# Two-layer hybrid decoder: retention products from rounded parts, and a reordered first feed-forward chunk

## The reference, cut to what matters

```
for i in range(2):
    x += mixer_i(rms_norm(x))                  # i = 0: retention, i = 1: attention
    x += relu(rms_norm(x) @ W_up)**2 @ W_down  # 1024 -> 4096 -> 1024

# retention, for each of 4 heads (q, k: 256 features, v: 512), in chunks of C = 128 tokens
scores = einsum('bnihd,bnjhd->bnhij', qc, kc) * dmat      # within a chunk
intra  = einsum('bnhij,bnjhe->bnihe', scores, vc)         # scores times v
def step(S, xs):
    cross = einsum('bihd,bhde->bihe', qi * q_dec, S)      # q times the state
    S = S * c_dec + einsum('bjhd,bjhe->bhde', ki * k_dec, vi)   # k times v
o = intra + cross;  o = o * rsqrt(mean(o*o) + eps);  o = o * silu(g);  return o @ w_out, S
```

## Time and profile before

| What | Value |
|---|---|
| Median of 3 executions | 2858.24 us |
| The profiled execution | 2859.83 us |
| Its span in the profile | 2858.0 us |
| TensorE matmul busy | 2804.2 us (98%) |
| VectorE busy | 1492.0 us (52%) |
| ScalarE busy | 801.7 us (28%) |
| Mean granted TensorE clock | 0.994 of full speed |

### The profile page before, as it was taken

One profiled execution on the slowest core, in us unless ns is written; L12 is line 12 of the kernel. 1 busy time (PEld: TensorE's weight loads), 2 busy tenths in 40 slices (PEclk: granted clock), 3 DMA queues, 4 the chain that ended last, 5 costly groups with the idle time before them and its releaser, 6 DMA issues.

```text
span 2858.0 us, 44910 instructions
## 1 busy us (share of the span) xinstructions
PE 2804.2 (98%) x18248; PEld 2645.0 (93%) x18248; DVE 1492.0 (52%) x2008; ACT 801.7 (28%) x1462; POOL 147.2 (5%) x114
## 2 busy tenths in 40 slices
PE   8999999999999999999999999998999999999999
PEld 8779959978996999999999999985799999999999
DVE  6443444434344577545554475456557744555554
ACT  3231132123113333223332242135423322233222
POOL 0000000000000110000000012124320000000000
PEclk9999999999999999999999999999999999999999
DMA  3232041122204111111111112230011111121112
GB/s 134 74 111 62 30 148 61 45 82 95 62 30 148 41 45 47 43 44 59 51 44 36 55 52 79 68 93 16 9 51 41 49 44 48 44 59 44 48 40 90
DMA packets 91241, 173.26 MB, mean 61 GB/s; under 512 B 9936, under 2 KB 15312, under 8 KB 90448
## 3 DMA queue, kind: packets, MB, share of 16 engines
q1 hardware_dynamic: 89200, 166.10, 18.2%
q10 hardware_dynamic: 1920, 5.41, 0.8%
HBM read 142.54 MB, written 25.56 MB: 59 GB/s over the span
## 4 chain that ended last, share of the span: by engine, by line
PE 93%; DVE 4%; ACT 1%; issue 1%; DMA 1%; POOL 0%; SPq 0%; ACTq 0%; DVEq 0%
PE ps L1641 61%; PE ps L1889 20%; PE ps L1782 2%; PE ps L1777 2%; PE ps L1681 1%; PE ps L2121 1%; PE ps L1788 1%; PE ps L2094 1%; DVE wlo L992 1%; PE ps L2105 1%; PE ps L1809 1%; ACT e_a L912 1%; PE ps L1765 1%; PE ps L1750 1%; PE ps L1822 0%
## 5 line engine op out<-in xcount | busy, mean ns | idle before, releaser
L1030 DVE TENSOR_TENSOR x<-ps,x 128x1056 f32<-128x1056 f32 x168 | 211.1, 1256 | 510.9 <-PE ps L1641 510.9
L1641 PE MATMUL ps<-ahi,whi 128*128 128x352 f32 x1920 | 415.1, 324 | 4.8 <-DVE x L1030 3.9
L1641 PE MATMUL ps<-alo,whi 128*128 128x352 f32 x1920 | 415.5, 324 | 0.0
L1641 PE MATMUL ps<-hhi,whi 128*128 128x352 f32 x1824 | 400.7, 328 | 12.6 <-DVE hlo L1000 8.9
L1641 PE MATMUL ps<-ahi,wlo 128*128 128x352 f32 x1920 | 412.0, 323 | 0.0
L1641 PE MATMUL ps<-hlo,whi 128*128 128x352 f32 x1824 | 396.2, 325 | 0.0
L1641 PE MATMUL ps<-hhi,wlo 128*128 128x352 f32 x1824 | 393.1, 324 | 0.0
L763 ACT CAST whi<-wraw 128x512 fp32r<-128x512 f32 x252 | 156.0, 619 | 628.8 <-PE ps L1641 440.0
L1641 PEld LDWEIGHTS ps<-ahi,whi 128*128 128x128 f32 x1920 | 325.3, 188 | 7.6 <-issue 3.7
L1641 PEld LDWEIGHTS ps<-ahi,wlo 128*128 128x128 f32 x1920 | 328.0, 189 | 0.0
L1641 PEld LDWEIGHTS ps<-alo,whi 128*128 128x128 f32 x1920 | 326.6, 187 | 0.0
(11 more groups left out here) (211 smaller groups left out, 3321.9 us busy)
## 6 DMA issues: line engine op xcount, KB each, us to landing
wraw<-in_weights SPq DMA_DIRECT2D x424, 256.0 KB, 2.6
s<-in_state_in SPq DMA_DIRECT2D x32, 512.0 KB, 4.1
out_state_s<-s SPq DMA_DIRECT2D x32, 512.0 KB, 3.7
zr<-z_a ACTq DMA_DIRECT2D x40, 132.0 KB, 2.4
x<-in_xT SPq DMA_DIRECT2D x8, 528.0 KB, 8.0
rope_tab<-in_tables SPq DMA_DIRECT2D x4, 1056.0 KB, 5.1
out_yT<-x SPq DMA_DIRECT2D x8, 528.0 KB, 2.7
out_state_p<-s_ret SPq DMA_DIRECT2D x4, 512.0 KB, 3.8
```

The lines of the kernel that those rows point to most:

```text
L1030: dve.tensor_tensor(blocks(x[:, k, :]), bank_set(m), blocks(x[:, k, :]), ALU.add).then_inc(mt_free, 1)
L1641: mm = pe.matmul(ps[:, 3 * (m % 2) + t, 0:TB], a[:, slot, w], b[:, s * KG + k, t * TB:(t + 1) * TB], start=(first and j == 0), stop=(last ...
```

## The change

In the chunk stage v, the masked scores and the decayed keys are kept as rounded high and low parts, and k times v and scores times v are made as three `fp32r` products each instead of one float32 product. VectorE makes the new parts: the low parts of v behind the v products (`keep_v_low`), those of keys and scores in `decay_keys`. v's last tile is turned into banks 0 and 1 (`v_bank`). The gate gets its own tile `gate_q` in v's place, and `o_t` moves to the place of q and k. In the last chunk `inverse_rms` comes before `update_samples`. In the first feed-forward chunk the forming work of tile 3 moves ahead of its relu, on VectorE and ScalarE.

```diff
-        v_tok = at("v_tok", o_v, [P, CH, DV], F32)
+        v_hi = at("v_hi", o_v, [P, CH, DV], F32R)
+        v_lo = at("v_lo", o_ahi, [P, CH, DV], F32R)
+        gate_q = at("gate_q", o_v, [P, 4, TOK], F32)
...
+        o_t = qk
...
+        def v_bank(e, half):
+            return half if e == 3 else 6 + half
@@ SyncE, ret_head: before the rotary table is loaded
-                    sp.wait_ge(ot_kept, h * (CH + 1))
+                    sp.wait_ge(a_lo, h * 4)
@@ ScalarE, keep_v
-                    act.copy(v_tok[:, 4 * half:4 * half + 4, e * P:(e + 1) * P],
-                             ps[:, 6 + half, :].rearrange("p (c f) -> p c f", c=4)).then_inc(v_kept, 1)
+                    act.copy(v_hi[:, 4 * half:4 * half + 4, e * P:(e + 1) * P],
+                             ps[:, v_bank(e, half), :].rearrange("p (c f) -> p c f", c=4)).then_inc(v_kept, 1)
@@ ScalarE, first_chunk
-                    else:
+                    if m in (1, 2):
                         form_hi(f, 2 * m - 2)
                         form_hi(f, 2 * m - 1)
...
                     act.copy(ahi[:, m, :], a2[:, m % 2, :]).then_inc(a_hi, 1)
+                    if m > 1:
+                        form_hi(f, 2 * m)
+                        form_hi(f, 2 * m + 1)
@@ VectorE, decay_keys
-                dve.tensor_scalar(k_tok[:, c % 2, :], ps[:, score_bank(c), 0:DK], kdec, None, ALU.mult
-                                  ).then_inc(kt_kept, 1)
...
+                dve.tensor_scalar(k_hi[:, c % 2, :], keys, kdec, None, ALU.mult).then_inc(dve_seq, 1)
+                dve.wait_ge(dve_seq, h * N_SEQ + seq[0] - 1)
+                dve.tensor_copy(sc_hi[:, c % 2, :], sc_t[:, c % 2, :]).then_inc(dve_seq, 1)
+                dve.wait_ge(dve_seq, h * N_SEQ + seq[0] - 1)
+                dve.scalar_tensor_tensor(out=k_lo[:, c % 2, :], in0=keys, scalar=kdec, in1=f32(k_hi[:, c % 2, :]),
+                                         op0=ALU.mult, op1=ALU.subtract).then_inc(kt_kept, 1)
+                dve.wait_ge(dve_seq, h * N_SEQ + seq[0])
+                dve.tensor_tensor(sc_lo[:, c % 2, :], sc_t[:, c % 2, :], f32(sc_hi[:, c % 2, :]), ALU.subtract
+                                  ).then_inc(sc_kept, 1)
+            def keep_v_low(h, e):
+                for half in range(2):
+                    high = v_hi[:, 4 * half:4 * half + 4, e * P:(e + 1) * P]
+                    dve.wait_ge(v_kept, h * 9 + (2 * e + half + 1))
+                    dve.tensor_tensor(v_lo[:, 4 * half:4 * half + 4, e * P:(e + 1) * P],
+                                      ps[:, v_bank(e, half), :].rearrange("p (c f) -> p c f", c=4), f32(high), ALU.subtract
+                                      ).then_inc(v_low, 1)
@@ VectorE, ret_head
+                    if m > 5:
+                        keep_v_low(h, m - 6)
                     read_normed(m, n + (2 * m + 2), tmp[:, m - 4, :])
...
+                keep_v_low(h, 2)
+                keep_v_low(h, 3)
                 mask_scores(h, 0)
                 decay_keys(h, 0)
...
-                    update_samples(h, c)
+                    if c + 1 < CH:
+                        update_samples(h, c)
                     inverse_rms(h, c)
+                update_samples(h, CH - 1)
@@ VectorE, first_chunk, tiles m = 0 to 3
-                        form_lo(f, 2 * m - 2)
-                        form_lo(f, 2 * m - 1)
-                    form_first(f, m)
+                    if m in (1, 2):
+                        form_lo(f, 2 * m - 2)
+                        form_lo(f, 2 * m - 1)
+                    elif m == 3:
+                        form_lo(f, 6)
+                        form_lo(f, 7)
+                    if m < 3:
+                        form_first(f, m)
+                    if m == 2:
+                        form_lo(f, 4)
+                        form_lo(f, 5)
+                        form_first(f, 3)
@@ VectorE, first_chunk, output tile m = 0
                         squares_lo(3)
-                        form_lo(f, 6)
-                        form_lo(f, 7)
@@ TensorE, turn_v
-                    if e:
-                        pe.wait_ge(v_kept, h * 9 + (2 * e + half - 1))
-                    elif half:
+                    if e in (1, 2):
+                        pe.wait_ge(v_low, h * 8 + (2 * e + half - 1))
+                    elif half and e == 0:
@@ TensorE, keys_and_scores, c == 0
-                    pe.wait_ge(v_kept, h * 9 + 7)
+                    pe.wait_ge(v_low, h * 8 + 5)
@@ TensorE, chunk
+                if c == 0:
+                    pe.wait_ge(v_low, (h + 1) * 8)
                 for j in range(2):
-                    mm = pe.matmul(ps[:, j, :], k_tok[:, c % 2, j * P:(j + 1) * P], v_tok[:, c, :],
-                                   start=True, stop=True)
+                    pe.matmul(ps[:, j, :], k_hi[:, c % 2, feats], v_hi[:, c, :], start=True, stop=False)
+                    pe.matmul(ps[:, j, :], k_hi[:, c % 2, feats], v_lo[:, c, :], start=False, stop=False)
+                    mm = pe.matmul(ps[:, j, :], k_lo[:, c % 2, feats], v_hi[:, c, :], start=False, stop=True)
...
-                pe.matmul(ps[:, bank, :], sc_t[:, c % 2, :], v_tok[:, c, :], start=(c == 0), stop=True
+                pe.matmul(ps[:, bank, :], sc_hi[:, c % 2, :], v_hi[:, c, :], start=(c == 0), stop=False)
+                pe.matmul(ps[:, bank, :], sc_hi[:, c % 2, :], v_lo[:, c, :], start=False, stop=False)
+                pe.matmul(ps[:, bank, :], sc_lo[:, c % 2, :], v_hi[:, c, :], start=False, stop=True
                           ).then_inc(o_done, 1)
```

More of the change, by code:

```diff
@@ L157, in trunk @@
         sc_t = at("sc_t", o_r + 4096, [P, 2, P], F32)
-        k_tok = at("k_tok", o_r + 5120, [P, 2, DK], F32)
+        k_tok = at("k_tok", o_r + 5120, [P, DK], F32)
+        k_hi = at("k_hi", o_r + 5120, [P, 2, DK], F32R)
         o_tok = at("o_tok", o_r + 7168, [P, DV], F32)
@@ L167, in trunk @@
         k4 = at("k4", o_r + 11072, [P, 2, 4, 4, NS // 4], F32)
-        v4 = at("v4", o_ahi, [P, 4, 4, 4, NS // 4], F32)
-        o_t = at("o_t", o_ahi, [P, 4, TOK], F32)
+        v4 = at("v4", o_work + 54048, [P, 4, 4, 4, NS // 4], F32)
+        o_t = qk
+        sc_hi = at("sc_hi", o_work + 58528, [P, 2, P], F32R)
+        sc_lo = at("sc_lo", o_work + 59552, [P, 2, P], F32R)
+        k_lo = at("k_lo", o_work + 60576, [P, 2, DK], F32R)
         tmp = at("tmp", o_alo, [P, 4, TOK], F32)
@@ L276, in trunk @@
         v_kept = sem("v_kept")
+        v_low = sem("v_low")
         four_ready = sem("four_ready")
@@ L735, in ret_head @@
                     act.wait_ge(mt_free, mt + (8 + m + 1))
-                    act.activation(qk[:, 2 + m % 2, :], qk[:, m % 2, :], ACT.Silu).then_inc(g_silu, 1)
+                    act.activation(gate_q[:, 2 + m % 2, :], gate_q[:, m % 2, :], ACT.Silu).then_inc(g_silu, 1)
                     act.wait_ge(g_of, h * 4 + (m + 1))
-                    act.copy(ahi[:, m, :], qk[:, m % 2, :]).then_inc(a_hi, 1)
+                    act.copy(ahi[:, m, :], gate_q[:, m % 2, :]).then_inc(a_hi, 1)
                 for m in range(DT):
@@ L1042, in _ @@
                 dve.tensor_tensor(ssum[:, :], ssum[:, :], sq[:, k % 2, :], ALU.add).then_inc(sum_done, 1)
-            N_SEQ = 12 + (CH + 1) + 3
+            N_SEQ = 12 + (CH + 1) + 3 + 3 * CH
             seq = [0]
@@ L1075, in mask_scores @@
                     dve.wait_ge(o_done, h * (CH + 1) + (c - 1))
-                dve.tensor_tensor(sc_t[:, c % 2, 0:rows], ps[:, score_bank(c), DK:DK + rows],
-                                  hmask[:, P:P + NS] if c == CH else hmask[:, 0:P], ALU.mult).then_inc(sc_kept, 1)
+                ins = dve.tensor_tensor(sc_t[:, c % 2, 0:rows], ps[:, score_bank(c), DK:DK + rows],
+                                        hmask[:, P:P + NS] if c == CH else hmask[:, 0:P], ALU.mult)
+                if c == CH:
+                    ins.then_inc(sc_kept, 1)
+                else:
+                    ins.then_inc(dve_seq, 1)
+                    seq[0] += 1
             def decay_keys(h, c):
@@ L1194, in gate @@
                     dve.wait_ge(ot_kept, (h + 1) * (CH + 1))
-                    dve.tensor_tensor(qk[:, m % 2, :], qk[:, 2 + m % 2, :], o_t[:, m, :], ALU.mult).then_inc(g_of, 1)
+                    dve.tensor_tensor(gate_q[:, m % 2, :], gate_q[:, 2 + m % 2, :], o_t[:, m, :], ALU.mult
+                                  ).then_inc(g_of, 1)
                 def gate_lo(m):
@@ L1731, in turn_v @@
                         t = (4 * half + c) * P
-                        mm = pe.transpose(ps[:, 6 + half, c * P:(c + 1) * P], tmp[:, e, t:t + P], ident)
+                        mm = pe.transpose(ps[:, v_bank(e, half), c * P:(c + 1) * P], tmp[:, e, t:t + P], ident)
                     mm.then_inc(v_turned, 1)
```

16 lines of the change are left out of this document (10 added, 6 removed).

## The result

| | Before | After |
|---|---|---|
| Median of 6 executions each | 2853.72 us | 2840.73 us |
| The profiled execution | 2859.83 us | 2841.45 us |
| Its span | 2858.0 us | 2839.7 us |
| Mean granted TensorE clock | 0.994 | 0.997 |

The ratio after to before is 0.9947, with a 95% interval of 0.993 to 0.9963: the kernel became 0.53% faster, 15 us (11 to 20), just beyond the 0.5% that the measurement can tell from no change. This is the ratio of the means of the six executions; the two medians lie 13.0 us apart. The median of before has moved from 2858.24 to 2853.72 us with three more executions, so part of the closeness of the forecast 2842 is luck; beside the timed experiments it was 2855.6 (17 executions) and 2856.1 (9). What the sum of the prediction is worth is read in the traces, term by term.

A forecast was written before the change was run, and what follows sets the result against it. TensorE, 93% of the chain that ended last, was taken as the bound. Chunk stages (13.8 us) plus feed-forward (2.6) gave 16.4, so 2859.8 becomes 2843.4, or 2842 us at the median; own range 2837 to 2847, 8 in 10 2835 to 2851.

The forecast's parts named there:

- the sum of the prediction: Whole kernel: 13.8 us from the chunk stages of four heads plus 2.6 from the feed-forward chunks, 16.4 us saved.
- both ranges: Whole kernel's time: the forecast's own range 2837 to 2847 us, and the 8 in 10 range 2835 to 2851.
- The fp32r product: Chunk stage, TensorE: an fp32r product of 512 columns takes 0.235 us, three 0.705 against 0.86 for one float32 product.
- VectorE's row: Odd chunks: three added operations delay the samples' update to +2.50 us, losing 0.10 to 0.15; odd chunks gain 0.34.
- Even chunks: Chunk stage: VectorE is ready in time, the whole 0.46 us arrives, and periods come near 6.56 us.
- the three additions: VectorE in a chunk: rounded scores and the low parts of keys and scores add 1.1 us (0.85 to 1.7).
- The start: Chunk 0: first k times v 0.75 us later, mostly recovered by cheaper products and idle time; net 0 on average per head.
- The end: Last chunk, scores times v to first gate product: shrinks by 0.6 us (0.3 to 0.8), to about 4.3.
- One head: Chunk stage of one head: odd chunks 1.0, even 1.4, chunk 0 nothing, chunk 7 0.9; say 3.45 us gained.
- The feed-forward chunk: First feed-forward chunk: fourth low part's wait unchanged, wait for the addition to `x` 1.44 to 0.2; gain 1.3 us per layer.
- VectorE as a bound: Rival, 25%: VectorE bounds odd chunks (0.4 us late each) and the start (0.5 each); about 2849 us.
- The slower clock at starts and ends: Rival, 4%: TensorE's clock falls, 1.5 us each; eight starts and ends cost 12 us and leave 2854, more make it slower.

The follow-up runs named there:

- e8: Changed kernel without the product of the scores' low part with v; even chunk periods 6.30 us, odd ones 5.61.
- e7: Changed kernel with the low part of the next scores made behind the samples' update; odd periods 5.54 us (5.61), even ones 6.53.
- e9: Changed kernel, second half of v's tile 3 in bank 3, its low part made behind chunk 0's parts; stages 0.31, 0.03, 0.27, 0.21 us shorter.
- e10: Changed kernel with the samples' update again ahead of the inverse root in the last chunk; stages 0.73, 0.66, 0.52 and 0.51 us longer.
- e1: Changed kernel with the feed-forward order of before on VectorE and ScalarE; ratio to before 0.996 (0.9944 to 0.9976).
- e2: Kernel before the change with only the new feed-forward order; ratio to before 0.9991 (0.998 to 1.0001).
- e4: Changed kernel with TensorE's loop over heads 1 to 3 written out as straight code; 2835.66 us in one execution.
- e3: Changed kernel with only low parts 4 and 5 ahead of the feed-forward relu of tile 3; relu of tile 2 to second chunk 63.44 us (62.99).
- e6: Changed kernel with the second-half low part of v's tile 2 made behind chunk 0's keys and scores; stages 53.90, 54.16, 54.15, 54.15 us, unmoved.
- e5: As e3, with ScalarE's casts of low parts 6 and 7 behind its cast of weight slab 8; relu of tile 3 to second chunk 50.50 us.

## Why the prediction was right, point by point

The forecast was 2842 us, 0.57% faster; measured 2840.73 us, 0.53% faster by the means, inside both ranges. By its own steps:

- **The fp32r product, 0.235 us: right.** 0.23 to 0.24 in the trace, 0.23 by leaving one out (e8). The Trainium skill, "TensorE: Matmul & The Clock Gate", section "Back-to-back issue gap", gives 216 ns as the gap of a product by itself, which the prediction took, and about 131 ns for a stream of weight loads and products. Neither is seen here: with new weights for each product the rows stay at 0.23 to 0.24 us.
- **VectorE's row: right to 0.02 us, its price too high.** The update starts at 127.97 - 125.45 = +2.52 (predicted +2.50), and VectorE does set the odd chunks (e8). But the loss is 0.07 by e7, not 0.12: 5.61 us instead of 5.68. Even chunks 6.54 against 6.56. The 1.1 us that the sum calls the three additions run from the start of the keys to the samples' update (126.85 to 127.97, 1.12 us); the additions alone take 0.73.
- **The start: the delay right (+0.78, predicted +0.75), the net 0.09 us of loss per head on average where 0 was put down.** Behind the last copy of v the queries start at 7.04, 7.11, 7.11 and 7.11 us, before at 6.80, 7.03, 7.24 and 6.93: +0.24, +0.08, -0.13, +0.18. The mechanism holds too: in before the queries start 0.13 us behind the landing of the second load of the samples' states in all four heads. But the idle time there was smaller than the rest of the delay in three heads, so that after the change k times v and not the load sets their start, and e9 could get some back.
- **The end: 0.75 in the first head instead of 0.6, but 0.50, 0.48 and 0.59 in the others, 0.58 on average.** 4.14 us where 4.3 was predicted, then 4.32 or 4.33; the order of the root and the update makes all of it (e10).
- **One head: 3.45 predicted, 3.50 measured; four heads 13.8 and 14.0.** The prediction's parts add up to 3.3: odd chunks 1.0, even ones 1.4, chunk 0 nothing, chunk 7 0.9. Measured 1.24, 1.45, -0.09 and 0.89; the odd chunks are the difference.
- **The feed-forward chunk: the step that failed.** "The second wait shrinks from 1.44 to about 0.2. Gain 1.3 per layer": measured 0.5. The relu is 1.75 us late, as predicted (1.7), and the second wait is gone. The step looked only at the two waits that were there. It did not ask who needs what stands behind the relu: `squares_lo(2)`, the third low part, had 0.40 us to spare (1.75 late, 1.35 waited). The three waits give 0.43 + 1.44 - 1.35 = 0.52 per layer, which is what the trace has. The fourth low part does come at the old time, but TensorE no longer waits for it, since it is late itself.
- **What no step had: +2.3 us** from the second gap in the loop of TensorE (e1, e2, e4).
- **Rivals.** VectorE as a bound is true of odd chunks, at 0.07 us and not 0.4. The slower clock at starts and ends did not come: the granted clock is 1.00 through all four stages of after, with a wait of 1.6 to 1.7 us ahead of the first k times v in each, and the fall behind head 3 in the earlier trace rows is absent. Its price was right: 1.45 us behind the last head of before and some 1.6 in e10, where 1.5 was put down. The Trainium skill, same page, section "HAM oscillation — how this bites in real kernels", speaks of gaps longer than any wait in these stages. The waits at the start agree with that; the three falls behind a wait of 1.39 us do not.

By its terms the sum was 16.4 us and the change's own part of the trace is 12.7: 0.2 too little in the stage, 1.6 too much in the feed-forward chunk, 2.3 of unforeseen cost. The fall of the clock that went, 1.45 us, would make it 14.1; no term had it. The measured 15 us (11 to 20) holds all three. The mechanism and the size of the main term are shown; that the time was met to 1.3 us is partly luck, since the median of before came out 4.5 us lower with more executions.

## What to carry to other kernels

When work moves ahead of a waiting instruction, list everything that stands behind that instruction and who needs it, with the slack of each: the wait that appears can be for a part that was never waited for. Removing one operation from a row on VectorE is worth nothing until the other inputs of the row (a copy on another engine, a turned tile) are known to be early; e3 and e6 gained nothing for that reason, and e5 and e9 did. Longer code in a loop was not free on the engine that is the bound: it cost 2.3 us in two passes here. And an idle time that looks small can be worth more than itself, if the clock falls behind it: look at the granted clock behind each wait.

## What the runs showed of the hardware that was not expected

A loop of TensorE over three heads cost 1.1 us at each return to its start in after (0.8 to 1.3 in the other traces with the loop), and a second gap of 0.6 to 1.3 us some 3 us behind it in every pass once the body had become longer; as straight code neither occurs, and with one product per chunk less the second doesn't (e8). The attention's time varies by 4.7 us between executions of the same instructions, with the number of falls to the lower clock (five in before and e3, at 135.8 us; two in after and e4, at 131.1), so a single span can't show a difference below that. Behind a wait of 1.39 us at the end of a head the clock fell in 3 of 12 heads, behind one of 0.66 us or less in none of 40, and a fall cost some 1.5 us. A wait of 1.6 to 1.7 us at the start of a stage brought none.
